# Gates of the first block regrouped, the last layer's end on 256 tokens, and products nobody reads set anew

## The reference, cut to what matters

```python
def token_mixer(h, w_in_l, w_out_l, conv_w_l, lbf, lbb, s0f, s0b, conv_fn):
    iv, zf, zb, q, g, cg, bg, hv = jnp.split(h @ w_in_l, SPLITS, axis=-1)
    o_rec, s_f, s_b = hgrn2_mix(q, iv, zf, zb, g, lbf, lbb, s0f, s0b)
    ...
def forget_terms(z, lb):
    f = lb + (1.0 - lb) * jax.nn.sigmoid(z)
    logf = jnp.log(jnp.maximum(f, F_FLOOR))
    key = (1.0 - lb) * jax.nn.sigmoid(-z)
    return logf, key
...
def second_block(x, meta_tokens, ...):
    meta = jnp.broadcast_to(meta_tokens[None].astype(x.dtype), (B, N_META, D_MODEL))
    h = jnp.concatenate([meta, x], axis=1)
    for i in range(DEPTH_2):
        kind, j = i % N_MIXERS, i // N_MIXERS
        y = rmsnorm(h, norm_mix[i])
        if kind == 0:
            mix = fox_mixer(y, fox_w_in[j], fox_b_f[j], fox_q_gain[j], fox_k_gain[j], fox_w_out[j])
        ...
        h = h + mix
        h = h + swiglu(rmsnorm(h, norm_ffn[i]), w_gate_up[i], w_down[i])
    return h[:, N_META:]
```

## Time and profile before

| | us |
|---|---|
| median of 3 runs (lowest to highest) | 4797.47 (4792.95 to 4807.65) |
| the profiled execution: its time, its span | 4795.78, 4793.9 |
| PE busy | 3998.1 (83%) |
| DVE busy | 3021.0 (63%) |
| ACT busy | 1904.1 (40%) |
| POOL busy | 1046.5 (22%) |

### The profile page before, as it was taken

How to read it: one execution, slowest core, us unless ns; L and a number is a source line. 1 busy time by engine, 2 the same in 40 slices (tenths; PEclk the granted TensorE clock), 3 DMA queues, 4 the chain that set the end, 5 groups by cost and what they waited for, 6 DMA issues and landing times. The chain is left out here.

```text
span 4793.9 us, 57677 instructions
## 1 busy us (share of the span) xinstructions
PE 3998.1 (83%) x20705; PEld 2891.5 (60%) x20705; DVE 3021.0 (63%) x6086; ACT 1904.1 (40%) x4163; POOL 1046.5 (22%) x950
## 2 busy tenths in 40 slices
PE   7894797777777777796877777799989999999999
PEld 3684673223232222385732322689979988898899
DVE  7567556676666666567666665556566573565564
ACT  7532323333333333442433333455434453444553
POOL 0006214444444444104144443000010003000000
PEclk9997899999999999997999999999999998999999
DMA  9420149999999999630699999325525540254254
GB/s 371 162 89 1 53 156 421 421 418 418 415 410 416 418 414 413 247 115 22 238 421 422 417 418 417 106 69 169 163 84 159 159 150 1 81 167 148 73 163 137
DMA packets 205630, 1143.70 MB, mean 239 GB/s; under 512 B 23952, under 2 KB 25488, under 8 KB 106528
## 3 DMA queue, kind: packets, MB, share of 16 engines
q0 software_dynamic: 110592, 805.36, 40.7%
q1 hardware_dynamic: 94752, 334.65, 21.7%
HBM read 1138.87 MB, written 1.05 MB: 238 GB/s over the span
## 5 line engine op out<-in xcount | busy, mean ns | idle before, releaser
L1313 PE MATMUL bank<-rows,diag 128*128 128x512 f32 x2304 | 1092.3, 619 | 368.4 <-ACT diag L1372 360.7
L409 PE MATMUL bank<-x_high,w_high 128*128 128x272 f32 (+3 forms) x3560 | 1108.7, 311 | 35.0 <-DVE x_low L494 18.6
L409 PE MATMUL bank<-x_high,w_low 128*128 128x272 f32 (+3 forms) x3560 | 1090.4, 306 | 0.0
L409 PE MATMUL bank<-x_low,w_high 128*128 128x272 f32 (+3 forms) x3560 | 1087.3, 305 | 0.0
L1313 PEld LDWEIGHTS bank<-rows,diag 128*128 128x128 f32 x2304 | 427.2, 195 | 1026.7 <-ACT diag L1372 572.3
L1419 DVE CUSTOM_DVE_ANT_0 junk<-rows,hT 128x1024 f32<-128x1024 f32 x576 | 705.8, 1225 | 412.1 <-DMA rows<-in_peer_uv,expert 396.0
L436 ACT CAST w_high<-ring 128x1024 fp32r<-128x1024 f32 (+2 forms) x541 | 555.5, 1029 | 883.6 <-PE bank L409 870.7
L479 DVE TENSOR_TENSOR w_low<-ring,w_high 128x1024 fp32r<-128x1024 f32 (+2 forms) x541 | 647.8, 1199 | 366.9 <-ACT w_high L436 365.6
L1269 POOL DMA_INDIRECT rows<-in_peer_uv,expert x576 | 618.1, 1073 | 1097.6 <-PE bank L1313 801.5
L409 PEld LDWEIGHTS bank<-x_high,w_high 128*128 128x128 f32 (+1 forms) x3560 | 675.2, 190 | 79.2 <-DVE x_low L494 25.4
L409 PEld LDWEIGHTS bank<-x_low,w_high 128*128 128x128 f32 (+1 forms) x3560 | 676.2, 190 | 22.7
(11 more groups left out here) (398 smaller groups left out, 4764.9 us busy)
## 6 DMA issues: line engine op xcount, KB each, us to landing
ring<-in_w_gate_up SPq DMA_DIRECT2D x176, 512.0 KB, 3.5
ring<-in_w_mod SPq DMA_DIRECT2D x96, 512.0 KB, 5.5
ring<-in_w_in SPq DMA_DIRECT2D x64, 512.0 KB, 3.5
ring<-in_fox_w_in SPq DMA_DIRECT2D x64, 512.0 KB, 3.5
ring<-in_w_down SPq DMA_DIRECT2D x64, 512.0 KB, 3.5
ring<-in_peer_wq SPq DMA_DIRECT2D x32, 512.0 KB, 3.5
ring<-in_gdn_w_in SPq DMA_DIRECT2D x32, 512.0 KB, 4.2
ring<-in_w_down SPq DMA_DIRECT2D x32, 384.0 KB, 3.7
```

What stands on the lines that cost most here:

```text
L409: last = pe.matmul(k.bank[c % outs_banks][0:m, 0:nt], w[:, slot, cols], xx[:, t, t0:t0 + nt], start=(t == 0 and n_pass == 0), stop=(t == K ...
L1313: last = pe.matmul(k.bank[2 * (i % 2) + half][:, :], diag[:, n % 4, :], slot(n)[:, D + half * 512:D + (half + 1) * 512], start=(e == 0), s ...
```

## The change

It has five parts.

1. **Gates.** The z chunks' units come first in `w_in`, the values behind them. The scaling by upper and lower goes from DVE to ACT (L746 and L747 of the new kernel), two of DVE's clamps are folded into others, the scans write their result where it is used, so that the copy falls away, and `low` is 8 buffers in a part of `proj` that is projected last. The steps' due numbers are new. DVE's feed is two instructions where there were five.
2. **The end of the last layer.** `fox_out` of the last layer, and its SwiGLU, run on 256 tokens and not on 272.
3. **The store.** Each of its 8 chunks is written by SP behind its eviction, inside the last stream; the stage `store` is gone.
4. **The meta tokens** are loaded inside the final norm's stage.
5. **Unread products.** 28 for 30 before the outputs' wait; 15 new ones at the outputs' end; 20 new ones at the end of gdn's head norm; 18 new ones at the end of gla's mix; in the fox attention 20 ahead of the wait for POOL and not 24 behind it, and 2 in each of three steps and not 4 in each of four.

```diff
     for l in range(DEPTH):
         chunks(a.w_mod[l], range(48))
     for l in range(DEPTH):
-        chunks(a.w_in[l], range(32))
+        chunks(a.w_in[l], (*range(4, 12), *range(4), *range(12, 32)))
         chunks(a.w_out[l], range(8))
         chunks(a.peer_wq[l], range(16))
     for i in range(4):
@@ -272,11 +272,15 @@
...
 
 
 
-    signals = "turned side_took sig keyed fed logs order summed"
-
-    def __init__(self, k, l, values, z, sums, gate):
-        self.k, self.l, self.values, self.z, self.sums, self.gate = k, l, values, z, sums, gate
-        self.low = values
+
+    signals = "turned side_took sig gated fed logs order summed"
+
+    def __init__(self, k, l, values, z, sums, low, gate):
+        self.k, self.l, self.values, self.z, self.sums, self.low, self.gate = k, l, values, z, sums, low, gate
 
     def pe(self, pe, s):
         k = self.k
         for c in range(HG_HEADS):
-            yield c + 2
-            pe.wait_ge(s.took, c + 1)
+            yield c + 10
+            pe.wait_ge(s.took, c + 9)
             if c >= 2:
                 pe.wait_ge(s.side_took, c - 1)
             for i in range(4):
@@ -729,66 +735,92 @@
             last.then_inc(s.turned, 1)
 
     def act(self, act, s):
-        k, z, sums = self.k, self.z, self.sums
-        for c in range(HG_HEADS):
-            yield c + 3
+        k, l, z, sums, low = self.k, self.l, self.z, self.sums, self.low
+
+        def gates(n):
+            upper, lower = k.upper[:, l, n:n + 1], k.lower[:, l, n:n + 1]
+            act.wait_ge(s.took, n + 1)
+            act.activation(sums[:, n, :], z[:, n, :], ACT.Sigmoid)
+            act.activation(z[:, n, :], z[:, n, :], ACT.Sigmoid, scale=-1.0).then_inc(s.sig, 1)
+            act.wait_ge(s.sig, n + 1)
+            act.activation(sums[:, n, :], sums[:, n, :], ACT.Identity, scale=upper, bias=lower).then_inc(s.gated, 1)
+            act.mul(z[:, n, :], z[:, n, :], upper)
+
+        def logs(n):
+            act.wait_ge(s.fed, n + 1)
+            act.activation(low[:, n, :], low[:, n, :], ACT.Ln, scale=2.0 ** 60)
+            act.activation(sums[:, n, :], sums[:, n, :], ACT.Ln).then_inc(s.logs, 1)
+
+        def turned(c):
             act.wait_ge(s.turned, c + 1)
             act.copy(k.v[:, :, c * P:(c + 1) * P], k.bank[SIDE_BANKS[c % 2]][:, :].rearrange("p (i d) -> p i d", i=4)).then_inc(s.side_took, 1)
-        for n in range(2 * HG_HEADS):
-            yield n + 6
-            act.wait_ge(s.took, n + 5)
-            act.activation(sums[:, n, :], z[:, n, :], ACT.Sigmoid).then_inc(s.sig, 1)
-            act.activation(z[:, n, :], z[:, n, :], ACT.Sigmoid, scale=-1.0).then_inc(s.keyed, 1)
-        load_tables(act)
-        for n in range(2 * HG_HEADS):
-            yield n + 15
-            act.wait_ge(s.fed, n + 1)
-            act.activation(self.low[:, n % 4, :], self.low[:, n % 4, :], ACT.Ln)
-            act.activation(sums[:, n, :], sums[:, n, :], ACT.Ln).then_inc(s.logs, 1)
+
+        for n in range(4):
+            yield n + 2
+            gates(n)
+        for n in range(4):
+            yield 7 + n // 2
+            if n == 0:
+                load_tables(act)
+            logs(n)
+        for n in range(4, 6):
+            yield n + 5
+            gates(n)
         for c in range(HG_HEADS):
-            yield c + 25
+            yield c + 11
+            if c < 2:
+                gates(c + 6)
+            turned(c)
+        for n in range(4, 8):
+            yield n + 10
+            if n == 4:
+                load_tables(act)
+            logs(n)
+        for c in range(HG_HEADS):
+            yield c + 21
             act.wait_ge(s.took, c + 17)
             act.activation(self.gate(c), self.gate(c), ACT.Silu)
 
     def dve(self, dve, s):
-        k, l, z, sums, low = self.k, self.l, self.z, self.sums, self.low
+        k, sums, low = self.k, self.sums, self.low
         order = Order(dve, s.order)
+        one = k.ones[:, 0:1].broadcast_to([P, SEQ])
+        first, second = slice(0, SEQ), slice(SEQ, TWO)
 
         def feed(n):
-            dve.wait_ge(s.sig, n + 1)
-            order(dve.tensor_scalar(sums[:, n, :], sums[:, n, :], k.upper[:, l, n:n + 1], k.lower[:, l, n:n + 1], ALU.mult, ALU.add))
-            order(dve.tensor_scalar(low[:, n % 4, :], sums[:, n, :], 1e-20, 2.0 ** 60, ALU.max, ALU.mult))
-            dve.tensor_scalar(low[:, n % 4, :], low[:, n % 4, :], 1.0, None, ALU.min)
+            dve.wait_ge(s.gated, n + 1)
+            dve.tensor_scalar(low[:, n, :], sums[:, n, :], 1e-20, 2.0 ** -60, ALU.max, ALU.min)
             dve.tensor_scalar(sums[:, n, :], sums[:, n, :], 2.0 ** -60, None, ALU.max).then_inc(s.fed, 1)
-            dve.wait_ge(s.keyed, n + 1)
-            dve.tensor_scalar(z[:, n, :], z[:, n, :], k.upper[:, l, n:n + 1], None, ALU.mult)
-
-        def run(n):
-            one = k.ones[:, 0:1].broadcast_to([P, SEQ])
+
+        def scan(n, cols):
+            return dve.tensor_tensor_scan(sums[:, n, cols], one, low[:, n, cols], 0.0, ALU.mult, ALU.add)
+
+        def begin(n):
             dve.wait_ge(s.logs, n + 1)
-            order(dve.tensor_tensor(sums[:, n, :], sums[:, n, :], low[:, n % 4, :], ALU.add))
-            for t0 in (0, SEQ):
-                cols = slice(t0, t0 + SEQ)
-                last = dve.tensor_tensor_scan(low[:, n % 4, cols], one, sums[:, n, cols], 0.0, ALU.mult, ALU.add)
-            order(last)
-            if n < HG_HEADS:
-                last = dve.tensor_copy(sums[:, n, :], low[:, n % 4, :])
-            else:
-                dve.tensor_copy(k.back_total[:, n - HG_HEADS:n - HG_HEADS + 1], low[:, n % 4, TWO - 1:TWO])
-                last = dve.tensor_tensor(sums[:, n, :], sums[:, n, :], low[:, n % 4, :], ALU.subtract)
-            last.then_inc(s.summed, 1)
-            dve.wait_ge(s.summed, n + 1)
-
+            order(dve.tensor_tensor(low[:, n, :], sums[:, n, :], low[:, n, :], ALU.add))
+            return scan(n, first)
+
+        def end(n):
+            last = scan(n, second)
+            if n >= HG_HEADS:
+                order(last)
+                order(dve.tensor_copy(k.back_total[:, n - HG_HEADS:n - HG_HEADS + 1], sums[:, n, TWO - 1:TWO]))
+                order(dve.tensor_tensor(sums[:, n, :], low[:, n, :], sums[:, n, :], ALU.subtract))
+
+        for n in range(4):
+            yield n + 4
+            feed(n)
         for n in range(4):
             yield n + 9
-            feed(n)
-        for n in range(4):
-            yield n + 17
-            run(n)
+            begin(n)
+            end(n)
+            yield n + 11
             feed(n + 4)
         for n in range(4, 8):
-            yield n + 18
-            run(n)
+            yield 2 * n + 7
+            begin(n)
+            yield 2 * n + 8
+            end(n)
...
-                fill(k, pe, 30, 0)
+                fill(k, pe, 28, 0)
...
             last.then_inc(s.sums, 1)
+            fill(k, pe, 15, BANKS - 1)
...
-                return dve.tensor_copy(values[:, c, :] if c < 4 else proj[:, c - 4, t0:t0 + n], bank[:, 0:n])
+                at = c if c < 8 else c - 4
+                return dve.tensor_copy(values[:, c - 8, :] if c in range(8, 12) else proj[:, at, t0:t0 + n], bank[:, 0:n])
...
-            side = HgrnSide(k, l, values, proj[:, 0:8, :], H, gate)
+            side = HgrnSide(k, l, values, proj[:, 0:8, :], H, proj[:, 20:28, :], gate)
...
-def project_residual_2(k, name, x, n_units=1, split_x=None):
-
-    stream(k, name, [(n_units, P, 0, T2)] * KD, x,
-           lambda dve, c, bank, s: dve.tensor_tensor(k.Y[:, c, :], bank[:, 0:T2], k.Y[:, c, :], ALU.add),
-           split_x=split_x, tables=True)
+def project_residual_2(k, name, x, n_units=1, split_x=None, t0=0, out=None):
+
+
+    T = T2 - t0
+
+    def sp_end(sp, s):
+        for c in range(KD):
+            sp.wait_ge(s.took, c + 1)
+            sp.dma_start(out[:, c, :], k.Y[:, c, t0:T2]).then_inc(k.stored, 16)
+        sp.wait_ge(k.stored, 16 * KD)
+
+    stream(k, name, [(n_units, P, 0, T)] * KD, x,
+           lambda dve, c, bank, s: dve.tensor_tensor(k.Y[:, c, t0:T2], bank[:, 0:T], k.Y[:, c, t0:T2], ALU.add),
+           split_x=split_x, tables=True, sp_end=None if out is None else sp_end)
...
+            pe.wait_ge(s.logged, len(chunks) - BANKS + 1)
+            fill(k, pe, 20, 0)
...
-    project_residual_2(k, "fox_out", H[:, :, 0:T2])
+    t0 = META if j == 1 else 0
+    project_residual_2(k, "fox_out", H[:, :, t0:T2], t0=t0)
...
         def _(pe):
+            fill(k, pe, 20, BANKS - 1)
             pe.wait_ge(s.cleared, 4)
-            fill(k, pe, 24, BANKS - 1)
...
-                if 1 <= n <= 4:
-                    fill(k, pe, 4, BANKS - 1)
+                if 1 <= n <= 3:
+                    fill(k, pe, 2, BANKS - 1)
...
                 last.then_inc(s.summed, 1)
+                fill(k, pe, 18, BANKS - 1)
...
-def swiglu(k, gain):
+def swiglu(k, gain, t0=0, out=None):
...
```

(5 more changed lines are left out.)

49 lines of the change are left out of this document (25 added, 24 removed).

## The result

The changed kernel takes 4772.96 us at the median of 11 runs (4761.84 to 4791.13), the kernel before 4799.29 (4792.95 to 4807.65): a ratio of 0.9945 with an interval of 0.9935 to 0.9954, 26 us less. That is half of the 53 us forecast, and outside the range. The profiled execution is the fastest of the 11 (4761.84), so its trace shows 34 us less than the profiled one of before.

The account below looks back on a forecast made before the run. No engine is full, so the bound changes from stage to stage. The terms 22.3 + 6.8 + 9.0 + 9.0 + 3.6 + 2.5 = 53.2 us give 4742.6, stated as 4744 us; range 4730 to 4767.

Parts of the forecast that it names:

- no unit over 6 us: Sign of being right: in `w_in`, no unit of 512 columns over 6 us behind the first.
- the last 20 units of layer 1: Sign of being right in `w_in`: these units take about 61 us, 58 and the 3 left.
- 22.3: Gates term in `w_in`: closing the holes gains 4.6 us in layer 0 and 17.7 in layer 1.
- Layer 0's 4.6: First hole of layer 0's `w_in`: three 512-column units go from 20.90 to 16.3 us.
- 6.8 forecast: Stages' ends: unread products keep PE's clock up in the four output projections, 6.8 us gained of at most 7.5.
- The 5.27 us: PE's idle time before layer 0's `w_out`, into which fifteen new unread products of 3.6 us were to fit.
- If PE then stays at 2.4 GHz: Condition at the stages' ends, despite gaps of some 2 us: 1.7 + 2.0 + 2.0 + 1.8 = 7.5 us go.
- The lower bound (-2): Worst case at the stages' ends: nothing gained and each stage's end 0.5 us later.
- I put 1.4 us for it. 4.5 each, 9.0 for both; bounds 2 and 5.9 each.: Fox attentions: first minimum 3.8 us earlier, 2.1 from fewer products in steps, less 1.4 for a low clock.
- clock not kept: Rival: gaps drop the clock, both attentions start long at 1.2 GHz; 6.8 and 4 us lost, 4755; chance 0.13.
- 9.0 forecast: Last layer: 1776 products lose 16 columns, 6.7 + 2.3 us gained; bounds 4 and 11.7.
- 3.6 and 2.5 forecast: Meta stage before the final norm goes, 3.6 us; the split store at the end lands 2.5 us sooner.

Follow-up runs that it names:

- the repeat of the change: The changed kernel once more, unchanged, for a second profile: a single run, 4771.88 us.
- one wait: POOL's convolution starts only behind DVE's four additions, on the changed kernel with bridged attention starts and four unread products in four steps: 4734.79 us, 13 less than without it.

## Why the prediction was wrong

- **Gates.** Right in the stream: no unit over 6 us, the last 20 units of layer 1 in 58.8 us (61 were forecast), the whole of `w_in` 2.7 and 19.0 us shorter. Alone the part brings 20 us for 22.3. Layer 0's 4.6 do not arrive: 1.8 go to PE's transpositions, which used to lie in the hole and now lengthen five units (29.0 us for 27.2), and the next stage gives 4.0 back. The forecast asked what is late next inside `w_in`, never what the new program does to the start of a stage in which two engines race.
- **Unread products at the stages' ends.** 6.8 forecast, 3 measured, from -1 to 7. In `gla_out` and `gdn_out` the clock is at 1.00 and 1.8 and 1.6 us are gained, near the 2.0 and 1.8 forecast. At `w_out` nothing is. PE there, after the change, against the earlier trace rows:

```profile
525.23 3.51 PE L162 MATMUL bank<-const 128*128 128x128 f32 x30
530.67 1.71 PE L162 MATMUL bank<-const 128*128 128x128 f32 x8 [1.92 <-PEq L129]
533.70 0.77 PE L415 MATMUL bank<-x_high,w_high 128*128 128x512 f32 x1 [1.31 <-DVE x_low L500]
```

  The 5.27 us were filled but for 1.92 us, a second pause of 1.31 us stayed behind them, and the first product still takes 0.77 us. The step "If PE then stays at 2.4 GHz" failed here: it took pauses of 0.36 and 0.55 us instead (22 products at the stage's end, 10 at `w_out`'s start) to have clock 1.00 and 43.8 us. The lower bound (-2) had allowed for it; the value taken had not.
- **Fox attention: the step that failed.** "I put 1.4 us for it. 4.5 each, 9.0 for both; bounds 2 and 5.9 each." The earlier start is there, 4.1 us. But the low clock costs a whole run of steps, so that each attention takes 3 us more than before: +6.0 us for both by the traces instead of -9.0, which is 15 of the 19 us that the profiled execution lacks. By the medians the part costs 14 or 17 us, so 23 to 26 of the 27 that are missing; of these the lines of the traces show 15. The forecast read that the clock fell behind 4.03 us of idleness, and put 1.4 us for the first steps, a price that no row gives. It did not ask which work the low stretch would fall on once the unread products had moved, nor how long it would last: about 7 us before, over while the 24 still ran, and about 20 now. What brings it back is not shown. The rival "clock not kept" had the right mechanism, at 4 us where the traces show 15, and gave it a chance of 0.13.
- **The last layer.** 9.0 forecast, 10.4 in the trace; the rows were the better guide than the figures of the Trainium skill (TensorE: Matmul & The Clock Gate, "Back-to-back issue gap"), 81 and 131 ns, by which the estimate was 3.7.
- **Meta and store.** 3.6 and 2.5 forecast, 3.8 and 4.3 (2.5 in the repeat of the change) and 3.3 in the traces; the last 128 KB land 2.0 us after their issue, where the megabyte took 4.8. The chunks do not go out one by one behind their evictions: SP's program reaches them only behind the last weights, and issues seven between 4749.9 and 4753.2 us and the eighth at 4756.2. Only the eighth had to wait for its eviction, so the end did not suffer. With the last layer they are 20 us for 15.1.
- **Range.** The parts' bounds summed reach to 4775, and the range was cut at 4767 because they would not all be at their worst. They were not: one part, the attentions, lies far outside its own bounds (2 to 5.9 us gained each, 3 lost), and its error is the same in both.

## What to carry to other kernels

Where an unread product is moved, say which stretch the low clock will then fall on: one that nobody waits for costs nothing, a chain of dependent steps cost some 7 us per attention here (74.1 against 67.3). Close every pause up to the first real product or leave the old ones alone, and use no more than the idle time holds; count again when the operand comes earlier. Before crediting a gain to a stage, look at the next one for engines that start together: 0.3 us of order between DVE and POOL cost 4 us here, and one wait gave back 13.

## What was not expected of the hardware

- Pauses of 1.68 and 0.73 us with work between them were followed by 17 to 21 us at 1.2 GHz in both attentions of both profiles of the change, while PE was busy 19.4 of 20 us by the profile. With the old fills in the changed kernel 3 us of near idleness at the same place of the first attention passed at 1.00, where in the kernel before they had not the earlier trace rows, and the clock fell later instead, among the steps, for 7 us; so such a fall is in part a matter of the moment:

```profile
3135.80:3138.80 3.00, 0.18 (x1) 1.00 0.01 3
```

- A DVE addition of 256 columns takes 0.35 us alone and 2.05 to 2.53 beside POOL; a multiplication of 1024 columns 1.2 alone and up to 2.9.
- The changed kernel's runs spread over 29 us, those of before over 15.
